# One-pass attention scores, a gate that multiplies the sums, and re-paced selection in a fused encoder step

## What is computed

```python
h = rms_norm(x) * (1 + scale1) + shift1;  z = h @ w_in            # q k v | B C X | gates
s = q @ k * HEAD_DIM**-0.5 + bias;  p = softmax(where(valid, s, -1e30));  att = p @ v
mixed = (sigmoid(ga) * (att @ w_o_att) + sigmoid(gb) * y_conv) @ w_o
x = x + gate1 * mixed
h2 = rms_norm(x) * (1 + scale2) + shift2
idx, g = product_key_top16(h2 @ w_pq, sub_keys1, sub_keys2)        # per head
u, v = expert_u[idx], expert_v[idx]
x = x + gate2 * sum_k(g * gelu(u . h2) * v)
```

## Time and profile before

| | us |
|---|---|
| median of 3 timed runs | 2015.4 (2012.54 to 2015.78) |
| the profiled execution's own time | 2008.13 |
| its span, first to last instruction | 2006.1 |
| busy: TensorE / VectorE / ScalarE / GpSimd | 1600.9 / 1203.8 / 721.4 / 621.1 |
| bytes moved | 718.22 MB |

### The profile page before, as it was taken

The page is one execution under the profiler, slowest core; times in us unless marked ns, Lnnn a source line. Parts: engine busy times, 40 slices in busy tenths (PEclk is TensorE's granted clock), DMA queues, the critical chain, the costliest instruction groups (busy, mean ns, idle before and its releaser), DMA issues.

```text
span 2006.1 us, 22251 instructions
## 1 busy us (share of the span) xinstructions
PE 1600.9 (80%) x7437; PEld 780.3 (39%) x7437; DVE 1203.8 (60%) x3104; ACT 721.4 (36%) x2231; POOL 621.1 (31%) x584
## 2 busy tenths in 40 slices
PE   6999998995868689979899677677677676767776
PEld 3775786853434345544455212112121121111221
DVE  2424212696888774444679857777766566664554
ACT  2215201344257633222534433333343333333332
POOL 0000000134332333423333534444434344334331
PEclk8999999997977789999999999898898999999999
DMA  9557520499987799999999999999999999999995
GB/s 399 204 184 274 203 105 22 190 377 366 421 350 281 306 397 412 411 414 410 413 403 378 411 422 421 422 421 422 422 421 421 422 421 422 421 421 421 422 421 245
DMA packets 100387, 718.22 MB, mean 358 GB/s; under 512 B 11489, under 2 KB 11505, under 8 KB 13489
## 3 DMA queue, kind: packets, MB, share of 16 engines
q0 software_dynamic: 82944, 604.02, 73.2%
q1 hardware_dynamic: 16464, 110.43, 14.1%
q10 hardware_dynamic: 864, 2.36, 0.3%
HBM read 712.04 MB, written 4.73 MB: 357 GB/s over the span
## 4 chain that ended last, share of the span: by engine, by line
DMA 45%; PE 30%; DVE 13%; issue 5%; ACT 3%; POOL 3%; SPq 0%; DVEq 0%; POOLq 0%; ACTq 0%
DMA ring<-in_expert_uv_dram,uidx 44%; PE ps L902 7%; PE ps L635 6%; DVE ring L1575 5%; PE ps L761 5%; POOL ring L503 3%; PE ps L782 2%; PE ps L820 2%; PE ps L767 2%; PE ps L631 1%; DMA ring<-in_wpack_dram 1%; PE ps L698 1%; PE ps L586 1%; PE ps L665 1%; PE ps L921 1%
## 5 line engine op out<-in xcount | busy, mean ns | idle before, releaser
L503 POOL DMA_INDIRECT ring<-in_expert_uv_dram,uidx x576 | 619.8, 1076 | 1301.5 <-PE ps L902 828.4
L1575 DVE CUSTOM_DVE_ANT_0 ring<-ring,mA 128x1024 f32<-128x1024 f32 x576 | 701.3, 1223 | 499.1 <-DMA ring<-in_expert_uv_dram,uidx 496.6
L902 PE MATMUL ps<-ring,wdiag 128*32 128x512 f32 x2304 | 777.6, 664 | 251.8 <-ACT wdiag L1164 180.4
L902 PEld LDWEIGHTS ps<-ring,wdiag 128*32 128x32 f32 x2304 | 162.8, 117 | 788.4 <-ACT wdiag L1164 432.2
L1157 ACT ACTIVATE gel<-act_in 128x1 f32<-128x1 f32 x576 | 116.7, 203 | 900.2 <-DVE act_in L1575 899.9
L1164 ACT ACTIVATE wdiag<-repeat,wsel 128x32 f32<-128x32 f32 x576 | 185.1, 321 | 18.9
L1159 ACT ACTIVATE wsel<-gel,gsel 128x1 f32<-128x1 f32 x576 | 169.6, 294 | 18.7
L635 PE MATMUL ps<-hB,ring 128*128 128x320 f32 x320 | 94.8, 446 | 6.5 <-DVEq L1332 5.8
L761 PE MATMUL ps<-hB,ring 128*128 128x320 f32 x256 | 80.4, 470 | 14.9 <-DVE kv L1396 10.6
L635 PE MATMUL ps<-hA,ring 128*128 128x256 f32 x320 | 72.3, 386 | 6.8 <-DVE qB L1289 3.7
L635 PEld LDWEIGHTS ps<-hB,ring 128*128 128x128 f32 x320 | 59.8, 194 | 35.8 <-issue 15.1
(11 more groups left out here) (241 smaller groups left out, 1593.1 us busy)
## 6 DMA issues: line engine op xcount, KB each, us to landing
ring<-in_wpack_dram SPq DMA_DIRECT2D x96, 1024.0 KB, 8.9
ring<-in_expert_uv_dram,uidx POOLq DMA_INDIRECT x576, 22.3
xB<-in_x_b_dram SPq DMA_DIRECT2D x2, 1280.0 KB, 19.2
o_y_p<-mA ACTq DMA_DIRECT2D x16, 128.0 KB
xA<-in_x_a_dram SPq DMA_DIRECT2D x1, 1024.0 KB, 4.9
bias<-in_bias_dram SPq DMA_DIRECT2D x1, 1024.0 KB, 31.9
o_v_p<-kv SPq DMA_DIRECT2D x4, 256.0 KB, 12.8
o_k_p<-xB SPq DMA_DIRECT2D x4, 256.0 KB, 7.8
```

The source lines that it names most:

```text
L503: nc.gpsimd.indirect_dma_start(out=ring[:, slot, :], out_offset=None, in_=ins["expert_uv"], in_offset=bass.IndirectOffsetOnAxis(ap=uidx[:, ...
L902: mm = nc.tensor.matmul(pY[c * GT:(c + 1) * GT, half, :], wdiag[:, n % NDIAG, :], ring[:, ROW[n][0], D + half * 512:D + (half + 1) * 512], ...
L1575: nc.vector.tensor_tensor_reduce(r, r, h2n[:, g % 2, :], 1.0, 0.0, ALU.mult, ALU.add, act_in[:, g % 2, j:j + 1]).then_inc(s["dot"], 1)
```

## The change

Three parts.

1. `bias_max`: the scale 1/8 goes into the gain of q once, at the start. Adding the bias and taking the maximum become one instruction (`tensor_tensor_reduce`), which writes minus the score and the running minimum; with more than 256 keys there are two, the second starting from the first one's minimum. The separate maximum and its semaphore `s_dve` go; the exponential uses scale -1.
2. Ends of tiles: `keep_sum` moves from ScalarE to VectorE and multiplies by the gate while it takes the sums, in two halves. `residual` comes ahead of `join`, and `join` accumulates onto it in PSUM. `scale` and `add` go; ScalarE copies the 32 finished rows (`result`). The first gate is prepared during tile 0.
3. Pacing: an `at` tick counts 1.25 in the spread of group 1's ticks. `pick(1)` is paced in three stretches: 12 steps in gathers 30 to 54, 8 in 55 to 98, 12 in 99 to 109; its end moves from gather 107 to 110.

```diff
+    cost = [1.25 if t[0] == "at" else 1.0 for t in left]
-        while done < len(left) and done * (PLACE_AT[2] - 8 - RUN) < (n + 1 - RUN) * len(left):
+        while done < len(left) and sum(cost[:done]) * (PLACE_AT[2] - 8 - RUN) < (n + 1 - RUN) * sum(cost):
...
+def fetch_of(kind, which):
+
+    at = [i for i, e in enumerate(ORDER) if e[0] == 1 and e[1][0] == kind][which]
+    return max(e[1] for e in ORDER[:at] if e[0] == "gather")
+
+
+BUSY = (fetch_of("at", 0) + 2, fetch_of("at", -1) + 2)
...
-                        pe.wait_ge(s[f"s_dve{g}"], u - 1)
+                        pe.wait_ge(s[f"mx{g}"], u - 1)
...
                     if j == 0 and g:
-                        pe.wait_ge(s["sum_kept"], g)
+                        pe.wait_ge(s["sum_kept"], 2 * g)
...
+                    if j == 7 and g:
                         join(g - 1)
-                    if j == 11 and g:
-                        residual(g - 1)
+                    if j == (13 if g else 29) and g in GATED:
+                        gate_rows(g)
...
+                    if j == 24 and g == NG - 1:
+                        residual(g)
...
-                    if first:
-                        cd.did(nc.vector.tensor_scalar(dst[:, 0:first], src[:, 0:first], HD ** -0.5, b[:, 0:1],
-                                                       ALU.mult, ALU.add))
-                    cd.did(nc.vector.scalar_tensor_tensor(dst[:, first:nk], src[:, first:nk], HD ** -0.5, b,
-                                                          ALU.mult, ALU.add))
-                    settle()
-                    dve.sem_inc(s[f"s_dve{g}"], 1)
-                    nc.vector.tensor_reduce(stat[0:w, u % 3, 0:1], dst[:, 0:nk], AX_X, ALU.max,
-                                            negate=True).then_inc(s[f"mx{g}"], 1)
+                    low = 3.0e38
+                    if first:
+                        cd.did(nc.vector.tensor_tensor_reduce(dst[:, 0:first], src[:, 0:first], b[:, 0:1].to_broadcast([w, first]),
+                                                              -1.0, low, ALU.add, ALU.min, stat[0:w, u % 3, 1:2]))
+                        settle()
+                        low = stat[0:w, u % 3, 1:2]
+                    nc.vector.tensor_tensor_reduce(dst[:, first:nk], src[:, first:nk], b, -1.0, low,
+                                                   ALU.add, ALU.min, stat[0:w, u % 3, 0:1]).then_inc(s[f"mx{g}"], 1)
...
+                def keep_sum(g):
+                    dve.wait_ge(s["fold"], GT * (g + 1))
+                    if g:
+                        dve.wait_ge(s["stored"], 16 * g)
+                    dve.wait_ge(s["gate_sb"], sum(x <= g for x in GATED))
+                    for half in range(2):
+                        cols = slice(half * 512, half * 512 + 512)
+                        nc.vector.tensor_tensor(prod[:, cols], pY[:, half, :], gate2[:, cols],
+                                                ALU.mult).then_inc(s["sum_kept"], 1)
...
-                PACE = [(1, RUN + 2, PLACE_AT[1] - 6, 32), (3, GT * FIRST[2] + 2, PLACE_AT[3] - 6, 32),
+                PACE = [(1, RUN + 2, BUSY[0], 12), (1, BUSY[0], BUSY[1], 8), (1, BUSY[1], PLACE_AT[1] - 3, 12), (3, GT * FIRST[2] + 2, PLACE_AT[3] - 6, 32),
```

More of the change, by code:

```diff
@@ L746, in merge @@
                     if q == 0 and d == 0:
-                        pe.wait_ge(s[f"s_dve{g}"], len(units(g)))
+                        pe.wait_ge(s[f"mx{g}"], len(units(g)))
                     if q == 0 and d:
@@ L905, in fold @@
                     mm.then_inc(s["fold"], 1)
[L907 to L914, removed]
                 def residual(g):
@@ L1165, in spread, with result @@
                                          scale=wsel[:, j:j + 1]).then_inc(s["diag"], 1)
[L1167 to L1171, removed]
+                def result(g):
+                    p, a = TILES[g]
+                    part = slice(a * GT, (a + 1) * GT)
+                    for half in range(2):
+                        act.wait_ge(s["joined"], 2 * g + half + 1)
+                        cols = slice(half * 512, half * 512 + 512)
+                        nc.scalar.copy(prod[part, cols], pG[part, cols]).then_inc(s["added"], 1)
                 def store(g):
                     p, a = TILES[g]
-                    act.wait_ge(s["added"], g + 1)
+                    act.wait_ge(s["added"], 2 * g + 2)
                     if p == 4:
@@ L1576, in dot @@
                                                    ALU.mult, ALU.add, act_in[:, g % 2, j:j + 1]).then_inc(s["dot"], 1)
-                def scale(g):
-                    p, a = TILES[g]
-                    part = slice(a * GT, (a + 1) * GT)
-                    dve.wait_ge(s["joined"], g + 1)
-                    if g in GATED:
-                        dve.wait_ge(s["gate_sb"], GATED.index(g) + 1)
-                    nc.vector.tensor_tensor(prod[part, :], pG[part, :], gate2[part, :], ALU.mult).then_inc(s["scaled"], 1)
-                def add(g):
-                    p, a = TILES[g]
-                    part = slice(a * GT, (a + 1) * GT)
-                    dve.wait_ge(s["natural"], g + 1)
-                    dve.wait_ge(s["scaled"], g + 1)
-                    nc.vector.tensor_tensor(prod[part, :], prod[part, :], pG[part, :], ALU.add).then_inc(s["added"], 1)
+                def keep_sum(g):
[3 more added lines that the diff above has]
+                    dve.wait_ge(s["gate_sb"], sum(x <= g for x in GATED))
+                    for half in range(2):
+                        cols = slice(half * 512, half * 512 + 512)
+                        nc.vector.tensor_tensor(prod[:, cols], pY[:, half, :], gate2[:, cols],
+                                                ALU.mult).then_inc(s["sum_kept"], 1)
                 def gather(n):
@@ L1597, in gather @@
                     g, j = m // GT, m % GT
-                    if j == 7 and g >= 1:
-                        scale(g - 1)
-                    if j == 14 and g >= 1:
-                        add(g - 1)
-                    for p, a, b, count in PACE:
-                        while a <= n < b and paced[p] * (b - a) < (n + 1 - a) * count:
+                    if j == 2 and g >= 1:
+                        keep_sum(g - 1)
+                    for i, (p, a, b, count) in enumerate(PACE):
+                        while a <= n < b and paced[i] * (b - a) < (n + 1 - a) * count:
                             next(ahead[p], None)
-                            paced[p] += 1
+                            paced[i] += 1
                     for p in range(1, 5):
-                        if n == PLACE_AT[p] - 6:
+                        if n == PLACE_AT[p] - (3 if p == 1 else 6):
                             next(ahead[p])
```

45 lines of the change are left out of this document (24 added, 21 removed).

## The result

| | before | after |
|---|---|---|
| median, us, 5 runs each on the same chip | 2013.54 | 2025.8 (2023.87 to 2030.56) |
| ratio, with its 95% interval | 1 | 1.0056 (1.0042 to 1.007) |
| the profiled execution's own time | 2008.13 | 2023.87 |
| its span | 2006.1 | 2021.7 |

The changed kernel is 11 us slower by the ratio (12 by the medians), where 19 us faster was forecast, and 2025.8 lies outside the range of 1982 to 2010. The profiled execution of before lies 5.4 us under its median and that of after 1.9 under its own, so the two profiles differ by 15.7 us, and some 4 us of what stretches show may be of the execution and not of the kernel.

What follows compares the result with a forecast made beforehand. Row DMA at 421 GB/s was taken as the bound, most loss in attention's VectorE-led lockstep. Terms -25.6 - 4.3 - 0.4 + 4.2 + 2.0 + 3.0 + 2.0 = -19.1 us gave 1996 us, range 1982 to 2010.

Steps and rivals of the forecast that it cites:

- part 2: Ends of tiles in the dense part: first folds 1.8 us later, seven times, half hidden; charged 2 us (0 to 10).
- a dip in the last third: Sign of being wrong: DMA below 421 GB/s there would mean the later product of a tile starves the ring.
- Attention: Gathers 55 to 98: fewer selection steps and cheaper scores shorten 149.6 us to 124, gain 25.6 (7.6 to 37).
- said to be the latest: Group 1's attention before the change: a lockstep in which VectorE is the latest most often and other engines wait.
- take over as a full engine: Attention after the change: ScalarE becomes the latest, 95.3 us of work, 7.9 us for each of 12 pairs.
- rival C: Attention stays in its lockstep: gain 4 to 8 us, chance 0.11; within 4 us of no change, 0.08.
- the floor of 133: Attention's least length, some 133 us, if each ScalarE table switch also drained 1.38 us; the sum about -11.
- Selection: Bunched steps and closer ticks: gathers 99 to 112 +4.2 us, 30 to 54 +2.0, from 113 on +3.
- One-pass scores: Group 1's attention: the 24 units' score work on VectorE falls from 28.7 to 18.9 us, saving 9.8 (1 to 10).
- The end of the kernel: Last tile: the store is issued 3.3 us after the last fold instead of 7.6, saving 4.3 (3.5 to 5).
- Rival D: Slower, 2022 us: attention keeps 3.40 us a gather, and 11.2 us given back outweigh the ends' 4.7; chance 0.07.

Runs made afterwards that it cites:

- ends_later: The kernel before with the new ends of tiles alone, the product behind dot 32g+6: 2080.27 us, ratio 1.034 to the kernel before.
- after_early: The changed kernel with the product of a finished tile behind dot 32g+2 instead of 32g+4: 2003.22 us, ratio 0.9953 to the kernel before.
- scores: The kernel before with the one-pass scores alone: 2004.0 us against 2011.76, ratio 0.9957.
- select: The kernel before with the three-stretch selection pacing alone: 2016.51 us against 2010.71, ratio 1.0026.
- early_no_select: The changed kernel with the product behind dot 32g+2 and selection in 32 even steps as before: 1996.09 us against the kernel before's 2009.06, ratio 0.9934.
- pace: The kernel before with the new pacing alone (attention ticks at weight 1.25, three-stretch selection): 2019.37 us against 2011.76, ratio 1.0039.
- ends_early: The kernel before with the new ends of tiles alone, the product behind dot 32g+2: ratio 0.9986 to the kernel before.
- ticks: The kernel before with attention ticks at weight 1.25 alone, selection paced as before: ratio 0.9997 to the kernel before.
- ends: The kernel before with the new ends of tiles alone, the product behind dot 32g+4: 2022.34 us against 2011.76, ratio 1.0051.

## Why the prediction was wrong

**The step that failed** is part 2: "Against the last of these folds, which needs dot 32g+3 anyway, that is about 1.3 (the next dot) + 1.4 - 0.9 (spread) = 1.8 us later, seven times in the dense part [...] I charge 2 us beyond the gain (0 to 10)". Part 2 alone costs 10.3 us net, and gains 4.3 at the end, so its ends in the dense part cost about 15; 13 of them go when the product stands at 32g+2, and in the whole change 21: outside the bounds. The charge did not follow from the working either, since 1.8 us for half of seven tiles is 6.3 and not 2. But the main mistake is in "the next dot". VectorE's order was counted by what it works, 1.3 us, but it waits there for a row to land; the 3.74 us ahead of dot 132 are that wait. The last weight of the four folds was ready at 822.75 and they start at 828.06, 5.3 us later where 1.8 was counted. The earlier trace rows had the DMA near its top in that stretch, where a row comes every 2.5 us and no sooner. With rows 32g+5 to 32g+7 alone under way behind it and four folds held back, the ring empties. "Half of the seven are hidden by the four rows still under way" took the slack as fixed, while the wait itself uses it up. That slower folds follow from TensorE's idling (3.67 us at a granted clock of 0.50, against 2.58 at 1.00 before) was no term at all. The prediction's own sign of being wrong, a dip in the last third, is faint in the kernel after (slices of 416 and 408), and from dot 235 to the last dot it takes 856.1 us against 855.9 before: 11 slots hid the wait there. It costs time only in `ends_later`. (Before, 421 GB/s begin at 1153 us and not at 1100: the slice from 1103 us has 411 in the earlier trace rows.)

**Attention**, the largest term: the loads were right (VectorE 87.6 us for 88.0 forecast, ScalarE 95.5 for 95.3) and the length wrong, 137.0 us for 124, near the upper bound of 142. It gained 12.6 us instead of 25.6, and not by the product's place (136.5 in `after_early`). It ended near rival C, with GpSimd's wait for folds still 72.1 us of the earlier trace rows's 92.2. The waits there:

```profile
POOL ring L513 <- PE ps L912: 72.1, 11, 10.8
DVE ring L1584 <- DMA ring<-in_expert_uv_dram,uidx: 29.6, 28, 3.7
ACT gel L1165 <- DVE act_in L1584: 21.6, 14, 2.9
ACT xB L1036 <- DVE stat L1371: 11.8, 9, 2.5
```

VectorE, said to be the latest, now waits 29.6 us for rows, and ScalarE's waits for it went down by 12 us, from 45.3 to 33.4. ScalarE did not take over as a full engine: 95.5 of 137.0. Nor does the length follow VectorE's load: with VectorE's work against the stretch, both in us, the kernels stand at 118.4 and 149.6 (before), 107.9 and 146.2 (`scores`), 107.5 and 154.5 (`select`), 106.9 and 142.6 (`early_no_select`), 99.2 and 142.3 (`pace`), 87.6 and 137.0 (after). The same 11 us off VectorE go with 3.4 us less or with 4.9 us more. What holds the stretch above its loads is perhaps a chain through all engines; no edit here removed a single link of it, and it stays open.

The Trainium skill (ScalarE: Activation LUTs, What ACT_TABLE_LOAD costs) gives a drain of about 1380 ns for every switch of tables beside the 1283 ns of the load. The trace does not agree: all 24 loads of the stretch take 1283 ns, and ScalarE has no more than 0.03 us of idle time ahead of any and 0.14 behind, as here:

```profile
603.88 0.32 ACT L1172 ACTIVATE wdiag<-repeat,wsel 128x32 f32<-128x32 f32 x1
604.22 1.28 ACT L1036 ACT_TABLE_LOAD   x1
605.51 0.61 ACT L1036 ACTIVATE xB<-xB,stat 128x384 f32<-128x384 f32 x1
```

So the 137 us are not the floor of 133 that the prediction worked out from that page. (By its own terms that floor would have made the sum -10, not -11.)

**Selection.** Gathers 99 to 112 took 50.1 us, 50 forecast. Gathers 30 to 54 took 84.5 against 77.4, +7.1 for +2.0: `after_early`, 79.0 us with the same selection, shows that 5.5 of it go with the product's place, at the tile's end behind gather 36. (`select` has 81.4 without the other parts, so the parts do not add up here.) Gathers 113 to 184 took +17.6 for +3. Bytes are not the reason here: length times GB/s is 94.8 MB for 93.8. The real term is the loss, 18.5 us less 3.2, and 4.3 of it go with the early place. What is left goes with part 3: with the early place the loss there is 14.2 us in `after_early`, 7.9 in `early_no_select` and 3.2 in `ends_early`, each by one profile. By which wait is not resolved.

**Right.** One-pass scores: 19.4 us for 18.9 forecast, by these groups of the kernel after between 575.6 and 712.6:

```profile
L1371 DVE CUSTOM_DVE_ANT_0 xB<-ps,bias,stat 128x256 f32<-128x256 f32 x16 | 7.7, 484 | 0.6
L1367 DVE CUSTOM_DVE_ANT_0 xB<-ps,bias 128x256 f32<-128x256 f32 x8 | 3.4, 421 | 6.5 <-PE ps L692 6.4
L1371 DVE CUSTOM_DVE_ANT_0 xB<-ps,bias 64x192 f32<-64x192 f32 x8 | 2.8, 348 | 6.9 <-PE ps L692 6.9
L1367 DVE CUSTOM_DVE_ANT_0 xB<-ps,bias 128x128 f32<-128x128 f32 x8 | 2.3, 287 | 2.4 <-PE ps L692 1.7 <-PE ps L675 0.7
L1367 DVE DVE_READ_ACCUMULATOR2_ANT stat<- 128x1 f32 x16 | 1.3, 84 | 0.0
L1371 DVE DVE_READ_ACCUMULATOR2_ANT stat<- 128x1 f32 x16 | 1.3, 84 | 0.0
L1371 DVE DVE_READ_ACCUMULATOR2_ANT stat<- 64x1 f32 x8 | 0.6, 75 | 0.0
```

The end of the kernel: the store is issued 3.3 us after the last fold, as forecast, where the earlier trace rows had 7.6:

```profile
2014.18 1.90 PE L912 MATMUL ps<-ring,wdiag 128*32 128x512 f32 x4 [0.55 <-ACT wdiag L1172]
2016.12 1.29 DVE L1594 TENSOR_TENSOR mA<-ps,mA 128x512 f32<-128x512 f32 x2 [2.91 <-PE ps L912]
...
2019.41 0.32 ACTq L1191 DMA_DIRECT2D o_y_s<-mA  x1
```

**Rival D** had the sign but not the reason: it has attention keep 3.40 us a gather and the selection pay, while attention came down to 3.11 and the tiles' ends paid.

**Open.** The parts measured singly are -8.6 (part 1), +10.3 (part 2), +5.2 (selection) and -0.6 (ticks), +6.3 us; the whole is +11.3. The 5 us between are no more than the five intervals leave open (some 5.5 us taken together, an estimate), and so are the 3 us between `pace`, +7.8, and its two halves, +4.6: that the parts make each other worse is not shown. The longer wait of TensorE for `kv` in the first output projection (11.5 us after, 4.7 before) is no candidate: it is 9.3 in `ticks` and 9.3 in `early_no_select`, of which the one loses nothing and the other has the lowest ratio. The early place has a price too: of the 4.3 us of the end `ends_early` keeps 2.8 (0.9986), and its gathers 55 to 98 take 157.4 us where `ends` has 150.1, while in the whole change the place moves that stretch by 0.5 us. Why is not known. Part 1's 8.6 us is also only partly placed: its attention stretch is 3.4 us shorter, and the profiled executions of `scores` and of before differ by 2.9 us in all.

## What to carry to other kernels

When work is put on an in-order engine behind an instruction that waits for a transfer, its price can be the transfer's landing and not the instruction's duration (3.74 us and 1.23 here): look for the idle time and its releaser ahead of that instruction, and put the work in front of it if its inputs are ready. Count how many slots stay in flight while the consumer is held, for beyond some delay the ring runs dry and the DMA loses time at each boundary: here 32g+2 and 32g+3 cost nothing that the times show, 32g+4 some 12 us, 32g+6 some 70. And where a change has several parts, time each alone: two of the three here hid a part that is worth 8.6 us.

## What the runs showed of the hardware

The one-pass minimum with a start value from memory (L1371) takes 484 ns for 256 columns, with a constant start value (L1367) 421 ns. L1367 also reads its bias as one repeated column; but L1371 itself, with its bias as a full tile, takes 421 ns where it starts from the constant, in group 0 (window 0 to 490 us), so the 63 ns go with the start value:

```profile
L1371 DVE CUSTOM_DVE_ANT_0 xB<-ps,bias 128x256 f32<-128x256 f32 x8 | 3.4, 421 | 6.4 <-PE ps L675 6.4
```

With one operand in PSUM and one in SBUF the form takes 287 ns for 128 and 421 for 256 columns, so 1.05 ns for each further column: one pass, as the dot of two SBUF operands. And the folds of four rows, 16 matmuls of 512 columns, took 3.67 us behind a stall of TensorE of 4.70 us, at a granted clock of 0.50, where four rows' folds of the same kernel at 788.03 us, at 1.00, take 1.94; all four weights were ready both times. The kernel before shows the same: 16 matmuls of 320 columns take 6.26 us behind 4.64 us of idle time (806.94 us; the granted clock is 0.50 from 808 to 810), and 4.57 us at 815.00, at 1.00. So these stalls cost once by their length and once more by the clock behind them.

ScalarE's table loads take 1283 ns and stand back to back with the instructions on both sides (the three rows above), 24 times in gathers 55 to 98.
